# One search tile handed from the projection to the attention, and the attention's tile order to match

## The reference, cut to what matters

```python
def indexer_scores(qi, wi, ki, q_pos, k_pos):
    dots = jnp.einsum('bqhd,bsd->bqhs', qi, ki)                    # 8 index heads of 64
    s = jnp.einsum('bqhs,bqh->bqs', jax.nn.relu(dots), wi * IDX_SCALE)
    return jnp.where(k_pos[None, None, :] <= q_pos[None, :, None], s, -jnp.inf)

def block(args):                                                   # 128 queries
    sc = indexer_scores(qib, wib, ki, q_pos, k_pos)
    _, idx = lax.top_k(sc, topk)                                   # topk = 256
    valid = idx <= q_pos[None, :, None]
    return sparse_attend(qb, gather_rows(k, idx), gather_rows(v, idx), valid)
```

## Time and profile before

| what | us |
|---|---|
| median of the three timed runs | 5218.58 |
| the profiled execution | 5226.54 |
| its span (first to last instruction) | 5224.8 |
| PE, DVE, ACT, POOL busy in the span | 4425.9, 2224.1, 1890.5, 577.9 |
| projection, first L754 product to last | 119.1 to 811 |
| attention's step 0 begins (first L1309 product) | 920 |
| attention's last residual stored | 2552 |

### The profile page before, as it was taken

How to read it: one execution, slowest core, us unless ns; L and a number is a source line. 1 busy time by engine, 2 the same in 40 slices (tenths; PEclk the granted TensorE clock), 3 DMA queues, 4 the chain that set the end, 5 groups by cost and what they waited for, 6 DMA issues and landing times. The chain is left out here.

```text
span 5224.8 us, 52692 instructions
## 1 busy us (share of the span) xinstructions
PE 4425.9 (85%) x15011; PEld 2234.9 (43%) x15012; DVE 2224.1 (43%) x5697; ACT 1890.5 (36%) x3264; POOL 577.9 (11%) x742
## 2 busy tenths in 40 slices
PE   7998886778999999898676699996999997699991
PEld 1443331223333333333335444442777774544440
DVE  1167775556555433232343410112566764611116
ACT  0145442766666632332112121221444443222223
POOL 0101011010010111112111000011000000210002
PEclk9999886789999999999776699997999998799995
DMA  8111101000000000000443677774112211568876
GB/s 294 50 49 40 35 31 64 7 15 9 15 15 5 20 18 15 26 26 21 150 154 129 262 289 281 271 255 148 48 67 73 73 41 64 189 209 298 293 260 274
DMA packets 153391, 598.18 MB, mean 114 GB/s; under 512 B 24823, under 2 KB 28791, under 8 KB 134216
## 3 DMA queue, kind: packets, MB, share of 16 engines
q1 hardware_dynamic: 105002, 426.61, 22.9%
q0 software_dynamic: 34208, 119.30, 6.5%
q10 hardware_dynamic: 13968, 49.73, 2.3%
HBM read 459.26 MB, written 136.38 MB: 114 GB/s over the span
## 5 line engine op out<-in xcount | busy, mean ns | idle before, releaser
L2523 PE MATMUL experts_ps_gu<-w_sb,experts_xT 128*128 x1504 | 681.8, 607 | 38.9 <-DMA w_sb<-moe_w_in 34.6
L1320 PE MATMUL attend_po<-attend_PT,V 128*128 128x512 f32 x1088 | 564.9, 644 | 49.9 <-ACT attend_total L1071 49.9
L754 PE MATMUL project_pj<-project_w,project_hT 128*128 128x512 f32 (+2 forms) x1360 | 542.7, 555 | 11.0 <-ACT project_hT L488 11.0
L3244 PE MATMUL recurrent_psAB<-recurrent_hT,rec_w_in_sb 128*128 128x256 f32 x2048 | 466.4, 381 | 0.8 <-ACT recurrent_hT L2920 0.8
L2523 PEld LDWEIGHTS experts_ps_gu<-w_sb,experts_xT 128*128 128x128 f32 x1504 | 285.7, 195 | 369.9 <-issue 369.8
L1061 ACT ACTIVATE attend_PT<-attend_big 128x512 f32<-128x512 f32 x544 | 294.0, 592 | 385.8 <-PE attend_big L1309 384.8
L3244 PEld LDWEIGHTS recurrent_psAB<-recurrent_hT,rec_w_in_sb 128*128 128x128 f32 x2048 | 389.4, 191 | 67.8 <-issue 17.2
L1153 DVE CUSTOM_DVE_ANT_0 attend_junk<-attend_aux,attend_hide 128x512 bf16<-128x512 f32 (+3 forms) x496 | 284.7, 614 | 266.2 <-issue 171.6
L754 PEld LDWEIGHTS project_pj<-project_w,project_hT 128*128 128x128 f32 (+1 forms) x1360 | 238.6, 196 | 296.5 <-issue 278.2
L1098 ACT ACTIVATE attend_passed<-attend_score,attend_cand 128x2048 bf16<-128x2048 f32 (+5 forms) x186 | 323.1, 1737 | 87.6 <-DVE attend_cand L1211 69.8
L2513 PE MATMUL experts_ps_y<-w_sb,experts_midT 128*128 x752 | 343.1, 599 | 11.4 <-issue 11.4
(11 more groups left out here) (578 smaller groups left out, 5832.2 us busy)
## 6 DMA issues: line engine op xcount, KB each, us to landing
w_sb<-moe_w_in SPq DMA_DIRECT2D x64, 2048.0 KB, 11.7
w_sb<-moe_w_in SPq DMA_DIRECT2D x64, 1024.0 KB, 8.5
yb_scratch<-experts_y ACTq DMA_DIRECT2D x94, 512.0 KB, 8.4
index_slab<-ada_w_in SPq DMA_DIRECT2D x12, 2048.0 KB, 14.6
hs_scratch<-route_h SPq DMA_DIRECT2D x32, 512.0 KB, 2.9
yb_scratch<-route_blank SPq DMA_DIRECT2D x32, 512.0 KB, 14.0
V<-ada_w_in SPq DMA_DIRECT2D x6, 2048.0 KB, 10.6
project_w<-attn_w_in_in SPq DMA_DIRECT2D x8, 1060.0 KB, 17.2
```

Source lines behind the costliest of these rows:

```text
L754: last = pe.matmul(pj[0:rows, (t * NCH + c) % BANKS, 0:c1 - c0], hT[:, b, k, 0:rows], w[:, k, c0:c1], start=(k == 0), stop=(k == KC - 1))
L1320: pe.matmul(po[:, n % 2, :], V1[:, b, n, :], PT[:, g % 4, :], start=(b == 0), stop=(b == S[i] // NKV - 1)).then_inc(pv_done, 1)
L2523: last = pe.matmul(ps_gu[:, u, :], xT[:, u, k, :], w1[:, bass.ds(slot, 1), k, :].rearrange("p a n -> p (a n)"), start=(k == 0), stop=(k == ...
L3244: last = pe.matmul(psAB[:, part, 0:WB], w_in[:, k, part * D + c * P:part * D + (c + 1) * P], hT[:, n // KC % 2, k, :], start=(k == 0), sto ...
```

## The change

Tile 9 is no longer an early tile (NPRE goes from 10 to 9). Its 24 index pieces and 37 rounds leave the projection, as do one store to and one load from `hides`; the segments of the searches of tiles 3 to 8 are set anew, most of them later and longer. In the attention tile 9 is late and is taken in falling order, after 10: its index pairs fall into step 5 and its rounds into step 6. The two tiles at the beginning are 6 and 8 instead of 7 and 9. The order becomes 6, 8, 15, 14, 13, 12, 11, 10, 9, 7, 5, 4, 3, 2, 1, 0. Buffers that are NPRE * 128 columns wide become narrower.

```diff
-NPRE = 10
+NPRE = 9
 EARLY = list(range(2, NPRE))
...
-    FIRST = dict(zip(EARLY, (40, 50, 62, 72, 88, 98, 116, 126)))
-    LAST = dict(zip(EARLY, (72, 82, 98, 108, 126, 136, 156, 166)))
+    FIRST = dict(zip(EARLY, (40, 50, 62, 74, 90, 104, 120)))
+    LAST = dict(zip(EARLY, (72, 84, 100, 114, 130, 146, 166)))
...
-        RAMP = [7, 9]
+        RAMP = [6, 8]
         TILE = RAMP + [t for t in range(NT - 1, -1, -1) if t not in RAMP]
```

## The result

The changed kernel takes 5208.28 us (median of 20 runs) against 5246.31 (20 runs of the kernel before). The ratio is 0.9948, with a 95% interval of 0.9925 to 0.9971: 0.5% faster, some 27 us, where 14 were predicted. One of the 20 runs of the changed kernel was disturbed (14664.99 us at a granted clock of 0.36); it is left out of the ratio and hardly moves the median. The profiled executions took 5226.54 us before and 5202.33 us after the change, with spans of 5224.8 and 5200.6. Up to the last residual that the attention stores, which is all that the change touches, the first has taken 2552.1 and the second 2529.7 us.

What follows compares the result with a forecast made beforehand. DVE was taken to bound projection tiles 6 to 13, rounds or PE the attention's halves. Projection -44 and attention +30 gave -14 us, 5204.6 against a median of 5218.6; range 5183 to 5234.

Steps and rivals of the forecast that it cites:

- Rival B: Projection: gives back PE's 15 us alone, shortening by less than 30; net +15, 5233.6 us; chance 0.15.
- The term for tile 13: Projection: tile 13, left without index pairs, goes from 57.9 to about 34 us, -24.
- The term for tiles 6 to 12: Projection: fewer additions and rounds on DVE give 18 us, taken as 16 because PE is close behind.
- that for tiles 14 to 16: Projection: 4 us back of the 13.3 above PE's floor of 91.5, as the last finish comes later.
- rival D: Projection: fewer stops in tiles 12 to 14 return half of 20 us of clock loss; net -24, 5194.6 us; chance 0.12.
- The opening: Attention before and in steps 0 and 1: fewer attended blocks and narrower units give -2, -4 and -4.5, sum -10.5 us.
- in the second halves PE decides: Attention steps 0 and 1: PE sets the second halves, so two blocks less shorten each by 4 us.
- Index and rounds of tile 9: Attention: index adds 11 us to step 5; rounds add 10.7 to step 6's first half, finish 0.5 to its second.
- Steps 7 to 9: Attention: PE's steps grow by 1, 9.5 and 8 us as later tiles change, sum +18.5, bounds 14 and 20.
- Rival C: Attention opening: steps 0 and 1 fall by 8 us each with PE's work; net -22, 5196.6 us; chance 0.12.
- E: Attention: fewer slots in step 6 and a delayed tile 9 mask cost another 12 us; 5216.6 us; chance 0.06.
- A: Whole kernel: the terms as summed, net -14 us, 5204.6 us; chance 0.55.

Runs made afterwards that it cites:

- the two narrowed kernels: Kernel before, projection only: index additions of heads 1 to 7 cut to 128 columns (projection 666.0 us), or index products of heads 2 to 7 to 128 keys (688.2).
- the second profiles: Both kernels profiled again with no edit: projection 691.5 us before and 637.8 after, attention 1744.8 and 1775.0.
- PE relieved: Kernel before, with the projection's index products of heads 2 to 7 taking only the first 128 keys of each piece: projection 688.2 us.
- tile 8 moved: Changed kernel with tile 8 also searched in the attention (NPRE = 8, order beginning 6, 7, new segments): ratio to before 0.9924.
- the three other profiles: Changed kernel with old segments, its attention alone behind the projection of before, and changed kernel with narrow relus for tile 14: attention 1771.7 to 1771.9 us.

## Why the prediction was right, and where its sum was off

**Sign and mechanism.** DVE's backlog sets the projection from tile 6 on, and relieving it shortens it by more than PE's share: shown from both sides by the two narrowed kernels, -25.6 us for 33 us less on DVE and -3.4 for 27 us less on PE. Rival B (only PE's 15 us come back, at a projection that shortens by less than 30) is out at -55.9 and -53.7.

**Projection, -44 predicted, -54 to -56 measured.** The term for tile 13 was 24 and is 26. (Its counts were off: by the tables tile 13 had 8 pairs and 25 rounds before, not 12 and 21. The term did not use them, as it was taken from the mean of tiles 14 to 16.) The term for tiles 6 to 12 was 16 and is 22, that for tiles 14 to 16 was 4 and is 7. How far DVE's relief shows depends on the segments: with the old ones it is 36 us, the other 18 to 20 come from the new ones. The sum also left out what it had handed to rival D: the clock in the projection rises as PE stops less. It is to be read on work that did not change. The L754 products, by the view of that one line over the projection, of before and of after:

```profile
119.10:810.70 691.60, 542.74 (x1360) 238.63 (x1360) 0.94 0.12 42
```

```profile
119.40:755.10 635.70, 531.77 (x1360) 235.80 (x1360) 0.96 0.13 44
```

The same 1360 products take 11.0 us less (7.0 between the second profiles, 542.3 and 535.3). D had asked for 10, and the miss of 10 to 12 us is about that. It is not an addition that can be separated cleanly, since PE's slower products partly lay under DVE's backlog. The Trainium skill, "TensorE: Matmul & The Clock Gate" (Part 1), prices lost clock at the throttled time times one half. The traces agree: of these products' busy time 53.5 us ran at 1.2 GHz before (counted from the traces' records of the granted clock), 36.8 after, 71.1 with PE relieved and 8.6 with tile 8 moved, and less half of that the four kernels' 542.7, 531.8, 551.5 and 516.1 us are 516.0, 513.4, 515.9 and 511.8.

**The opening, -10.5 predicted.** Before step 0 -2.1 (predicted -2). Steps 0 and 1 were to shrink by 4 and 4.5 and did by 0.1 and 0.9 (in the second profiles they grew by 2.7 and 0.5). The step that failed is "in the second halves PE decides": PE's 48.8 of 61.2 us in step 0 was read as if it were the 72.6 of 74.9 of step 4. The prediction had itself named an unchanged length of steps 0 and 1 as a sign of being wrong, and that sign came. What the traces show in its place is DVE with no pause over 0.11 us through 33 (before) and 35 us (after) of step 0's second half; the trace of before had that already. The first halves behaved as read: rounds set them, step 1's kept 87.5. (The terms given for step 0, -4, +2.7 and -2, make -3.3 and not -4.) What stands close behind DVE in the second half stays open. Less work on PE, on DVE or on ACT each left it within 2.4 us. That the engines pass it to one another in turn fits the waits for relus that grew from 1.7 to 8.9 us; no run here isolates it.

**Index and rounds of tile 9.** +11 predicted for step 5, 9.2 measured (its second half +9.7). +11.2 for step 6, 10.1 measured: the first half +12.0 rather than +10.7, the second -1.9 rather than +0.5. (Step 6 takes 119.9 us and not 122.5 in five of the other profiles with tile 9's rounds in it, +7.5.) Taking the next step's index or search as a price list worked, because the neighbouring steps do the same work.

**Steps 7 to 9.** +18.5 predicted, 16.1 measured between the first profiles, 10.5 between the second (step 7 105.5 to 106.4 us, step 8 88.1 to 94.9, step 9 76.2 to 79.0).

**Attention in all.** +30 predicted, +33.2 and +30.2 measured (27 to 31 by the three other profiles). That it is so close is luck in part: the missing 7 to 11 us of the opening are partly offset by 5 to 11 us in the later terms. Rival C (the opening shrinks with all of PE's work) is therefore out, and so is E (a dearer late search): step 6 takes 122.5 us. What the prediction had only in part is that the opening's cover is free: tile 7 in place of 6 there costs nothing and shortens the attention by 7 to 10 us.

**The net.** -14 predicted; -22 and -23 in the two pairs of profiles up to the last residual; -27 in the timed ratio, with 15 to 39 in its interval. The projection's term is the one that was mis-sized. In size D's -24 is nearer than A's -14, and D's reason, fewer stops and a higher clock, was there. The predicted 5204.6 us lie within 4 us of the measured median, and that is luck: they were reckoned from a median of 5218.58 us in three runs, where 20 runs have 5246.31. What made the median of before so low is chance; the last section says how much one execution can differ from another.

## What to carry to other kernels

When work is interleaved by a table, compare each stretch with the same stretch without the extra work (30.5 us a tile here) and with each engine's share. If the in-order backlog of an engine other than PE sets it, moving that work away gives back most of the backlog (36 us here, of 44 by the prediction's estimate), and spreading what remains can be worth half as much again (18 to 20 us here). Before trusting that an engine decides a stretch, ask for its busy share and for the pauses of the others: in halves where PE was busy 80 or 88% (steps 0 and 1), two blocks less, priced at 4 us, gave back 1.6 at most; in one at 96% (step 5) the index cost 9.7 us of the 11 priced. Where a search sets the time anyway, give it more to cover: here tile 7 was as free in step 0 as tile 6.

## What the runs showed of the hardware

The times of one and the same kernel fall in two groups, 5217 to 5231 and 5242 to 5261 us for before. One stretch that no kernel here changes, from the recurrent block's last L3244 product to the second experts' first L2523 product, shows where. First the profile of before, then that of before again:

```profile
4381.80:4553.50 171.70, 83.80 (x537) 70.51 (x536) 101.30 (x253) 42.71 (x63) 37.35 (x52) 0.71 0.45 161
```

```profile
4377.00:4580.80 203.80, 119.18 (x536) 107.13 (x535) 101.45 (x253) 42.01 (x63) 18.85 (x52) 0.55 0.38 136
```

The same instructions take 171.7 or 203.8 us, according to whether TensorE's clock comes back to 2.4 GHz in the middle of them (granted 0.71) or stays at 1.2 GHz nearly throughout (0.55). PE had been less than 60% busy in it in both. A part of the first with the clock back at 2.4 GHz (granted 1.00), and all of the second from the fall on (0.50):

```profile
4442.50:4490.20 47.70, 43.86 (x394) 42.26 (x392) 38.25 (x49) 31.07 (x43) 29.46 (x28) 1.00 0.85 304
```

```profile
4397.90:4580.80 182.90, 100.73 (x488) 98.79 (x488) 90.95 (x229) 37.35 (x55) 18.85 (x52) 0.50 0.43 151
```

Of all fourteen profiles eight had 171.6 to 173.7 us, five 203.8 to 204.3 and one 190.6. Why the clock comes back in one execution and not in another is not shown. It is worth 32 us in a run, more than this change, so stages of a profile, most of which repeat to 0.1 to 3 us, decide what medians of a few runs cannot. That the two groups of times are these two forms is a reading: the two profiled executions of before lie 25.6 us apart, and only profiled executions can be looked into. The profile of the kernel with tile 8 moved had the long form, and the changed kernel's the short one: their spans (5210.6 and 5200.6 us, the stretch 204.0 and 172.8 of them) are in the wrong order for that reason.
